# A decoder step with routed experts: the sample rows' expert choices summed by TensorE, already transposed

## The reference

```python
x = x + moe(rmsnorm(x, norm_ffn), ...)      # y = sum over 4 choices of weight * expert row (+ b_down)
x = x + jax.nn.sigmoid(x @ w_ple_gate) * (p @ w_ple_proj)
y = rmsnorm(x, norm_final)
```

## Time and profile before

| | before |
|---|---|
| median of 3 executions | 1432.5 us (1431.93 to 1433.74) |
| the profiled execution | 1430.52 us |
| its span, first to last instruction | 1428.7 us |
| mean granted TensorE clock | 0.992 |
| busy: PE, PEld, DVE, ACT, POOL | 98%, 80%, 88%, 66%, 17% |
| chain that ended last | PE 92%, DVE 3%, DMA 2%, issue 1%, ACT 1% |
| DMA moved | 457.34 MB, mean 320 GB/s |

### The profile page before, as it was taken

The page is one execution under the profiler, slowest core; times in us unless marked ns, Lnnn a source line. Parts: engine busy times, 40 slices in busy tenths (PEclk is TensorE's granted clock), DMA queues, the critical chain, the costliest instruction groups (busy, mean ns, idle before and its releaser), DMA issues.

```text
span 1428.7 us, 19602 instructions
## 1 busy us (share of the span) xinstructions
PE 1393.2 (98%) x6631; PEld 1146.8 (80%) x6631; DVE 1253.3 (88%) x1028; ACT 936.7 (66%) x634; POOL 240.4 (17%) x130
## 2 busy tenths in 40 slices
PE   7999998999999999999999999999999999999997
PEld 5898777888888888888888888888888888888665
DVE  5777388999999999999999999999999999999885
ACT  4313156777777777777777777777777777777522
POOL 3131000322222211111111111111111111111100
PEclk9999989999999999999999999999999999999999
DMA  7113378999999999999999999999999999999661
GB/s 263 60 63 102 118 295 299 338 363 372 381 369 372 370 383 371 371 371 369 371 368 370 369 375 369 373 366 381 368 373 376 370 373 373 371 372 365 201 234 59
DMA packets 94170, 457.34 MB, mean 320 GB/s; under 512 B 13314, under 2 KB 14894, under 8 KB 60213
## 3 DMA queue, kind: packets, MB, share of 16 engines
q1 hardware_dynamic: 84255, 437.50, 80.5%
q0 software_dynamic: 9360, 17.85, 3.3%
q10 hardware_dynamic: 526, 1.60, 0.5%
HBM read 451.76 MB, written 21.58 MB: 331 GB/s over the span
## 4 chain that ended last, share of the span: by engine, by line
PE 92%; DVE 3%; DMA 2%; issue 1%; ACT 1%; POOL 0%; POOLq 0%; DVEq 0%; ACTq 0%
PE ps L1382 47%; PE ps L1391 24%; PE ps L1235 4%; PE ps L1532 2%; PE ps L1398 2%; PE ps L1363 2%; PE ps L1370 2%; DMA expert_rows<-y_rows,scatter_col 2%; PE ps L1150 1%; PE ps L1152 1%; PE ps L1157 1%; DVE resid L2050 1%; PE ps L1260 1%; PE ps L1092 1%; PE ps L1095 1%
## 5 line engine op out<-in xcount | busy, mean ns | idle before, releaser
L1822 DVE TENSOR_TENSOR w_lo<-raw,w_hi 128x2048 fp32r<-128x2048 f32 x384 | 866.4, 2286 | 46.4 <-PE ps L1391 45.1
L929 ACT ACTIVATE w_hi<-raw 128x2048 fp32r<-128x2048 f32 x384 | 732.2, 1916 | 216.7 <-PE ps L1382 155.3
L1382 PE MATMUL ps<-w_hi,xT_hi 128*128 128x512 f32 x1024 | 277.7, 393 | 2.7 <-ACT w_hi L929 1.6
L1382 PE MATMUL ps<-w_hi,xT_lo 128*128 128x512 f32 x1024 | 274.5, 390 | 0.1
L1391 PE MATMUL ps<-w_lo,xT_hi 128*128 128x512 f32 x1024 | 273.8, 389 | 0.0
L771 POOL DMA_INDIRECT expert_rows<-y_rows,scatter_col x32 | 166.7, 5208 | 403.7 <-ACT y_rows L962 403.7
L1382 PEld LDWEIGHTS ps<-w_hi,xT_lo 128*128 128x128 f32 x1024 | 192.2, 188 | 41.6 <-DVE xT_lo L1878 0.5
L1391 PEld LDWEIGHTS ps<-w_lo,xT_hi 128*128 128x128 f32 x1024 | 192.3, 188 | 40.0
L1382 PEld LDWEIGHTS ps<-w_hi,xT_hi 128*128 128x128 f32 x1024 | 189.7, 188 | 41.2 <-ACT w_hi L929 2.0
L1382 PE MATMUL ps<-w_hi,aT_hi 128*128 128x512 f32 x512 | 140.0, 395 | 0.3 <-DVE token_of L1954 0.3
L1382 PE MATMUL ps<-w_hi,aT_lo 128*128 128x512 f32 x512 | 136.9, 389 | 0.0
(11 more groups left out here) (294 smaller groups left out, 1200.6 us busy)
## 6 DMA issues: line engine op xcount, KB each, us to landing
raw<-in_w_up_dram SPq DMA_DIRECT2D x256, 1024.0 KB, 6.6
raw<-in_w_down_dram SPq DMA_DIRECT2D x128, 1024.0 KB, 7.6
raw<-in_w_ple_gate_dram SPq DMA_DIRECT2D x4, 1024.0 KB, 5.5
yk<-expert_rows SPq DMA_DIRECT2D x4, 1024.0 KB, 8.0
raw<-expert_rows SPq DMA_DIRECT2D x4, 1024.0 KB, 6.4
resid<-in_x_prompt_dram SPq DMA_DIRECT2D x4, 512.0 KB, 7.5
w_v_sb<-in_w_in_dram SPq DMA_DIRECT2D x2, 1024.0 KB, 7.9
w_z_sb<-in_w_in_dram SPq DMA_DIRECT2D x2, 1024.0 KB, 12.7
```

The costliest lines, as they stand in the source:

```text
L929: act.activation(w_hi[:, s % SPLIT, :], raw[:, slot(s), :], ACT.Copy).then_inc(s_hi, 1)
L1382: mm = pe.matmul(out[:, c:c + 512], (xh, xl)[xs], w_hi[:, s % SPLIT, base + c:base + c + 512], start=(fresh and xs == 0 and base == 0), st ...
L1822: dve.tensor_tensor(w_lo[:, s % SPLIT, :], raw[:, slot(s), :], w_hi[:, s % SPLIT, :].bitcast(F32), ALU.subtract).then_inc(s_lo, 1)
```

## The change

A load of the sample's 128 expert rows (4 choices of 32 rows), one on each partition, goes ahead of all other loads of the tail. VectorE lays the choices' weights out as a 32x128 table with zeros elsewhere, TensorE transposes it between the last expert's products, and VectorE copies it out as 128x32. TensorE then makes the sample's transposed rows by itself: for each of eight column groups one product of the expert rows with the weights, and one of the residual's rows with the identity, summed in PSUM. This stands behind the last embedding and ahead of the last two bias sums, and takes the place of the sample's transposes. VectorE's four adds for the sample rows move behind the second tile's adds and the last bias adds, two ahead of the second tile's low part and two behind it. The buffers change turns: the third tile's rows go where the second's were, the fourth's where the sample's were, and SP waits accordingly.

```diff
             sp.wait_ge(s_scat, 16 * n_over + 16 * E)
+            sp.dma_start(y_sample_rows[:], y4_dram[LAST * P * TOPK:T * TOPK, :]).then_inc(s_ys, 16)
             for i, t in enumerate(TORD):
-                if i >= YB:
-                    sp.wait_ge(s_comb, i - YB + 1)
+                if i == 3:
+                    sp.wait_ge(s_comb0, 1)
+                elif i >= YB:
+                    sp.wait_ge(s_comb, i // YB)
...
+            def sample_x2():
+                pe.wait_ge(s_ys, 16)
+                pe.wait_ge(s_bd, 2)
+                for k in range(KD):
+                    cols = slice(k * P, (k + 1) * P)
+                    x2 = x2_bank(0)[:, k // 4, (k % 4) * P:(k % 4) * P + NS]
+                    pe.matmul(x2, y_sample_rows[:, cols], weight_cols[:], start=True, stop=False)
+                    mm = pe.matmul(x2, resid[0:NS, LAST, cols], ident[0:NS, 0:NS], start=False, stop=True)
+                mm.then_inc(s_x2tp, 1)
...
+                if c == 1:
+                    pe.wait_ge(s_wrow, 1)
+                    pe.transpose(ps[:, 7, 0:NS], weight_rows[:], ident[0:NS, 0:NS]).then_inc(s_wcolp, 1)
...
             tail_embedding(4)
+            sample_x2()
             b_down_sum(3)
...
-            x2_transposes(0)
...
+                    dve.tensor_tensor(weight_rows[:].rearrange("p (t k) -> p t k", k=TOPK),
+                                      ident[0:NS, 0:NS].rearrange("p (t o) -> p t o", o=1).to_broadcast([NS, NS, TOPK]),
+                                      topw[0:NS, LAST, :].rearrange("p (o k) -> p o k", o=1).to_broadcast([NS, NS, TOPK]),
+                                      ALU.mult).then_inc(s_wrow, 1)
...
+            dve.wait_ge(s_wcolp, 1)
+            dve.tensor_copy(weight_cols[:], ps[:, 7, 0:NS]).then_inc(s_wcol, 1)
...
-            combine(0)
             combine(1, range(1))
             x2_low(0)
             combine(1, range(1, TOPK))
             b_down_add(3)
             b_down_add(4)
+            dve.wait_ge(s_x2tp, 1)
+            combine(0, range(2))
             x2_low(1)
+            combine(0, range(2, TOPK))
```

More of the change, by code:

```diff
@@ L279, in build @@
             ple_rest = sb("ple_rest", [P, TT - 2, D], scope=s)
-            sb("unused_rows", [P, 2, D], scope=s)
+            y_sample_rows = sb("y_sample_rows", [P, D], scope=s)
+            sb("unused_rows", [P, D], scope=s)
             yk1 = sb("yk1", [P, TOPK, D], scope=s)
@@ L286, in build @@
             gate_hi = [sb(f"gate_hi{i}", [P, 2, D], F32R, scope=s) for i in range(2)]
-            sb("bias_picks", [P, 2, P], scope=s)
+            weight_rows = sb("weight_rows", [NS, P], scope=s)
+            weight_cols = sb("weight_cols", [P, NS], scope=s)
+            sb("bias_picks", [P, P - NS], scope=s)
             gate_hi += [sb("gate_hi2", [P, 2, D], F32R, scope=s), gate_hi3]
@@ L298, in build @@
         YB = 2
+        YBUF = (0, 1, 1, 0, 1)
+        YUSE = (1, 1, 2, 2, 3)
         YK = (yk0, yk1)
@@ L462, in build @@
         s_comb = sem("moe_added")
+        s_comb0 = sem("sample_moe_added")
+        s_ys = sem("sample_expert_rows_landed")
+        s_wrow = sem("sample_weight_rows_ready")
+        s_wcolp = sem("sample_weights_transposed")
+        s_wcol = sem("sample_weight_columns_ready")
         s_x2tp = sem("x2_transposed")
@@ L632, in _ @@
             y4 = y4_dram.rearrange("(t k) d -> t (k d)", k=TOPK)
+            sp.dma_start(y_sample_rows[:], y4_dram[LAST * P * TOPK:T * TOPK, :]).then_inc(s_ys, 16)
             for i, t in enumerate(TORD):
-                if i >= YB:
-                    sp.wait_ge(s_comb, i - YB + 1)
+                if i == 3:
+                    sp.wait_ge(s_comb0, 1)
+                elif i >= YB:
+                    sp.wait_ge(s_comb, i // YB)
                 for h in range(2):
-                    sp.dma_start(YK[i % YB][0:NT[t], 2 * h:2 * h + 2, :].rearrange("p k d -> p (k d)"),
-                                 y4[t * P:t * P + NT[t], h * 2 * D:(h + 1) * 2 * D]).then_inc(s_yk[i % YB][h], 16)
+                    sp.dma_start(YK[YBUF[i]][0:NT[t], 2 * h:2 * h + 2, :].rearrange("p k d -> p (k d)"),
+                                 y4[t * P:t * P + NT[t], h * 2 * D:(h + 1) * 2 * D]).then_inc(s_yk[YBUF[i]][h], 16)
                 if i == 1:
@@ L1508, in _ @@
             b_down_sum(1)
+            pe.wait_ge(s_wcol, 1)
             tail_embedding(3)
@@ L1518, in x2_transposes @@
                 n = NT[t]
-                pe.wait_ge(s_comb, i + 1)
+                pe.wait_ge(s_comb, i)
                 if i >= 2:
@@ L2045, in combine @@
                 x = resid[0:n, t, :]
-                yk = YK[i % YB][0:n]
+                yk = YK[YBUF[i]][0:n]
                 for k in ks:
                     if k % 2 == 0:
-                        dve.wait_ge(s_yk[i % YB][k // 2], 16 * (i // YB + 1))
+                        dve.wait_ge(s_yk[YBUF[i]][k // 2], 16 * YUSE[i])
                     ins = dve.scalar_tensor_tensor(out=x, in0=yk[:, k, :], scalar=topw[0:n, t, k:k + 1], in1=x,
@@ L2054, in combine @@
                     else:
-                        ins.then_inc(s_comb, 1)
+                        ins.then_inc(s_comb if i > 0 else s_comb0, 1)
             def x2_low(i):
```

## The result

The changed kernel takes 1438.7 us in the median of 5 executions (1437.8 to 1439.2), the kernel before beside it 1431.9 us. The ratio is 1.0046, with a 95% interval of 1.0035 to 1.0056. The prediction was 1436.9 us in a range of 1434.6 to 1438.8: slower as forecast, 1.8 us beyond the number and 0.1 us inside the upper end of the range. In the table of experiments one execution of 2370 us (g) and one of 8036 us (the kernel before, beside f, g and h) are left out.

A forecast was written before the change was run, and what follows sets the result against it. The end was taken to follow VectorE's third-tile adds: TensorE's sum puts the low part at 1364.4, 19.32 us of VectorE work end at 1383.7 against 1379.29, so 1432.5 + 4.4 = 1436.9 us, range 1434.6 to 1438.8.

The forecast's parts named there:

- What bounds: Tail: the end follows VectorE's adds of the third tile, or TensorE's later arrival there; behind it TensorE alone.
- The weight transpose: Between the last expert's products on TensorE: costs 0.11 to 0.53 us, taken as 0.25, shifting everything behind it.
- The landing: Second tile's first half of rows, ahead of VectorE's first add: lands 1.2 us later, at least 0.43, behind the new load.
- The sum on TensorE: Behind the last embedding: eight groups of 0.70 us, 5.6 us, plus 0.75 for a clock fall; decides VectorE's low part.
- "not slower" rival: TensorE's sum takes under 4.8 us, so the landing starts VectorE: end 1435.1 or 1434.1 us; chance 0.17.
- The clock stays up: Rival: no clock fall in TensorE's sum, which ends at 1363.14; end 3.7 us later, 1436.2 us; chance 0.15.
- VectorE without idle: VectorE from the sample's low part to the third tile's last add: 19.32 us of work with no idle left.
- the likeliest case: The clock falls once, in the last microsecond of TensorE's sum, about 0.75 us: end 1436.9 us; chance 0.45.
- the clock falls once more: Rival: TensorE's 2.6 us gap ahead of the third tile's transposes halves the clock behind it, 1.4 us: 1438.3; chance 0.18.

The follow-up runs named there:

- g: Changed kernel with three sample adds back ahead of the second tile's, TensorE's sum shape by shape, and the sample's low part ahead of the second tile: 1434.32 us, ratio 1.0012.
- f: Kernel before plus only the new 512 KB load ahead of the tail's other loads, read by nothing: 1433.59 us against 1432.00, ratio 1.001.
- h: As g, with the sample's sum between the last embedding's halves and ScalarE's copy of that embedding behind the sample's high part: 1433.15 us against 1432.00, ratio 1.0006.
- c: Changed kernel with SP issuing the second tile's two loads ahead of the sample rows' two: 1437.81 us against 1432.31 for the kernel before, ratio 1.0046.
- b: Changed kernel with TensorE's sum as eight 128-row products, then eight 32-row ones (output misses parts of the sum): 1434.98 us against 1432.31, ratio 1.0025.
- d: Changed kernel with eight unread gate products filling TensorE's wait ahead of the third tile's transposes: 1437.42 us against 1432.31 for the kernel before, ratio 1.004.
- a: Changed kernel with three sample adds back ahead of the second tile's, the fourth behind the sample's low part: 1434.47 us against 1432.31, ratio 1.0017.
- i: As h, but second tile's loads first on SP and its adds first on VectorE, sample adds behind: 1431.43 us against 1431.62 for the kernel before, ratio 1.0001.

## Why the prediction was right, and where it fell short

**What bounds.** Right: the end followed VectorE's adds of the third tile, and the tail behind the transposes was TensorE's own. The transposes started 0.05 us behind VectorE's last add, as 0.06 in the earlier trace rows.

**The weight transpose.** 0.18 us, inside 0.11 to 0.53 and near the 0.25 taken.

**The landing.** Too small. The first half of the second tile's rows came 1363.79 - 1353.63 = 10.2 us behind the first load's issue; before it was 1359.82 - 1351.87 = 8.0. So the new load costs 2.2 us rather than 1.2: I had sized it by the spacing of two landings of 512 KB behind each other, but the loads behind it became longer too: the sample rows' two took 5.0 us to land (median) instead of 3.7. It did not matter for the time: behind its first add VectorE still waited 1.41 us for TensorE's sum and ScalarE's copy, as the prediction had it, and in c an earlier landing gave nothing.

**The sum on TensorE.** Right in place and size. It started 11.43 us behind the first embedding, as the bias sums before (1357.29 - 1345.85 = 11.44); a group took 0.67 us ((1362.72 - 1359.36) / 5) for the 0.70 taken; the clock fell in it and cost 1.17 us for the 0.75 taken (6.53 - 8 x 0.67). The "not slower" rival rested on the router's rate, 0.106 us a record, and fell: with the shapes in turn a record took 0.168 us, and only shape by shape (b) 0.119. The Trainium skill, page "TensorE: Matmul & The Clock Gate" (Part 2), says that TensorE pulls weight loads ahead of running products when the row groups don't conflict or when the load goes to the background weight buffer. The prediction named only the first of these conditions; both shapes of the sum use the first 32 rows, so by rows the loads overlap the product ahead of them in every turn, and within a shape too. Whether the second condition accounts for the rates no run here shows.

**The clock stays up.** This rival fell, in all four profiles with the shapes in turn (changed, a, c, d). TensorE was busy for 4.00 of 4.00 us ahead of the fall at 1363, so no idle gap brought it on. The Trainium skill, same page (Part 1), puts the gate down to how busy TensorE has lately been; read as busy time in the profile (4.00 of 4.00 us), this trace disagrees with it.

**VectorE without idle.** Nearly. From the low part to the third tile I had 19.32 us; it took 19.97, with one wait of 0.96 us ahead of the second low part. I had said that the half clock in the gate products goes on a path that waits anyway. It didn't quite: bias sums and gate products took 1374.24 - 1365.89 = 8.35 us instead of 6.72, and TensorE's transposes, not VectorE, set that low part. This and the longer fall in the sum are the terms that were too small, 5.1 us at the third tile's transposes, and 0.18 for the weight transpose, instead of 4.4 in all.

**The step that failed** is the choice between the likeliest case and the rival "the clock falls once more". I gave that 0.18, priced it at 1.4 us, and left it out of the number; only the upper end of the range covered it. It came: a wait of 2.12 us (I had 2.6), then half clock for the transposes and most of 16 gate products, 1.62 us. In d it is absent, and the tail is 1.5 us shorter. With it, the prediction's own sum is 1438.3, 0.4 under the median. That this is so near is partly luck: the sum starts from 1432.5 where the kernel before measured 1431.9 beside the changed one, and its terms were about 1 us too small. Only one execution was profiled, with a mean granted clock of 0.988; two of the five have 0.990 and took 1437.8 us, so whether the second fall comes in every execution is open.

## What to carry to other kernels

An operation taken off a wait still has to be done somewhere: before moving it, look at what the engine does with its idle time in the place it goes to, because the adds that cost little ahead of a load's landing cost 1.8 us at the join (38.57 instead of 36.80 in a), and in the profile a fall of the clock behind it. Small products whose stationary operands alternate in rows are better issued shape by shape: 3.8 us instead of 5.4 here, at the same clock. When one engine's wait is removed, read the next join at once: in b, g and h each repair did its own part and brought out the next wait behind it.

## What was not expected of the hardware

- 16 + 16 records with 32 moving columns took 3.80 us shape by shape and, in turns, 0.67 us for each group of four, or 5.4 us at the same clock: each change between 128-row and 32-row stationary operands costs about (5.4 - 3.8) / 14 = 0.11 us, since there are 15 changes in turns and one shape by shape.
- In these profiles neither busy time alone nor the length of a gap alone tells where the clock falls. With the same 3.80 us of short products it stayed at 1.00 where long products stood on both sides (h and i, one execution each), and fell behind them in b and g. Behind a wait of 2.12 us ahead of the third tile's transposes it fell in the changed kernel and in c, behind one of 2.09 in b it didn't. What tips it was not settled.
- One unread 512 KB load ahead of the others delayed the sample rows' first add by 1.9 us and lengthened the kernel by 1.6 us in the median (f).
